# First mixer: steps in another order and banks dealt anew; second mixer: the last convolution taps behind the next tails

## What is computed

```python
h = _rmsnorm(x, norm_mix_pre)
z_a, z_b, z_c, z_d = _split(h @ w_in, GROUP_SPLITS)
y_a = _rwkv7(z_a, ...)   # 4 heads of 64: s = s*w + (s@-kk) x (kk*a) + v x k, y = s@r
y_b = _mlstm(z_b, ...)   # 4 heads, chunks of 64, gates from i_pre and f_pre
y_c = _swa(z_c, ...)     # window of 128, sinks, relative bias
y_d = _fox(z_d, ...)     # causal softmax with forgetting gates
x = x + _rmsnorm(concatenate([y_a, y_b, y_c, y_d]) @ w_out, norm_mix_post)
gate, up = split(_rmsnorm(x, norm_ffn_pre) @ ffn_w_up)
x = x + _rmsnorm((gelu(_causal_dwconv(gate)) * up) @ ffn_w_down, norm_ffn_post)
```

```python
q, k, v, g, a_lr, u, gate_b, gate_c = split(h @ w_in)
o = gla_chunked(q, k, v, logg) ...                    # four heads, chunks of 64
z = gate_b * causal_dwconv(gate_c * u, conv_w)        # three taps a channel
return concatenate([o, z]) @ w_out
```

## Time and profile before

| | |
|---|---|
| median of 3 runs | 1627.43 us |
| the profiled execution's own time | 1627.35 us |
| its span in the trace | 1625.6 us |
| PE busy | 1604.6 us (99%) |
| DVE busy | 823.2 us (51%) |
| ACT busy | 669.9 us (41%) |
| POOL busy | 266.4 us (16%) |
| chain that ended last | PE 95%, DVE 3%, DMA 1%, ACT 1%, issue 1% |

### The profile page before, as it was taken

One profiled execution on the slowest core, in us unless ns is written; L12 is line 12 of the kernel. 1 busy time (PEld: TensorE's weight loads), 2 busy tenths in 40 slices (PEclk: granted clock), 3 DMA queues, 4 the chain that ended last, 5 costly groups with the idle time before them and its releaser, 6 DMA issues.

```text
span 1625.6 us, 22612 instructions
## 1 busy us (share of the span) xinstructions
PE 1604.6 (99%) x8876; PEld 1318.4 (81%) x8876; DVE 823.2 (51%) x1403; ACT 669.9 (41%) x1227; POOL 266.4 (16%) x229
## 2 busy tenths in 40 slices
PE   9999999999999999999999999999999999999998
PEld 6776777888888888888888888878888888888887
DVE  6667557376555622374444433346775444443333
ACT  7556555464444333363333333244334433333222
POOL 1222122002222110002222210000020122222000
PEclk9999999999999999999999999999999999999999
DMA  5331100423323333223233332333223232332332
GB/s 189 93 92 41 54 27 14 145 89 104 96 88 101 101 94 98 85 90 104 91 101 94 99 96 85 110 102 104 66 79 104 91 104 91 96 99 89 95 106 75
DMA packets 45984, 149.59 MB, mean 92 GB/s; under 512 B 5260, under 2 KB 8500, under 8 KB 45880
## 3 DMA queue, kind: packets, MB, share of 16 engines
q1 hardware_dynamic: 41760, 142.10, 28.3%
q10 hardware_dynamic: 4120, 6.06, 1.1%
HBM read 146.03 MB, written 2.11 MB: 91 GB/s over the span
## 4 chain that ended last, share of the span: by engine, by line
PE 95%; DVE 3%; DMA 1%; ACT 1%; issue 1%; DVEq 0%; SPq 0%; ACTq 0%
PE bank L280 93%; PE bank L478 1%; DVE x L2324 1%; DVE lo L1829 0%; DMA raw<-in_w_in 0%; DVE x L2665 0%; DVE y L2319 0%; ACT hi L1116 0%; PE bank L530 0%; DMA raw<-in_ffn_w_gate 0%; PE bank L538 0%; DMA raw<-in_w_out 0%; DVE yf L2319 0%; DVE small L1962 0%; ACT sq L1250 0%
## 5 line engine op out<-in xcount | busy, mean ns | idle before, releaser
L1829 DVE TENSOR_TENSOR lo<-raw,hi 128x512 fp32r<-128x512 f32 (+1 forms) x514 | 393.7, 790 | 572.4 <-ACT hi L1116 572.2
L280 PE MATMUL bank<-xh,hi 128*128 128x512 f32 (+1 forms) x1640 | 618.2, 388 | 3.5 <-ACT xh L1528 1.3
L280 PE MATMUL bank<-xh,lo 128*128 128x512 f32 (+1 forms) x1640 | 608.2, 382 | 1.3 <-DVE lo L1829 1.2
L280 PE MATMUL bank<-xl,hi 128*128 128x512 f32 (+1 forms) x1592 | 598.3, 387 | 0.0
L1116 ACT ACTIVATE hi<-raw 128x512 fp32r<-128x512 f32 (+1 forms) x540 | 322.1, 616 | 423.2 <-PE bank L280 378.4
L280 PEld LDWEIGHTS bank<-xh,hi 128*128 128x128 f32 x1640 | 304.3, 189 | 72.3 <-issue 6.8
L280 PEld LDWEIGHTS bank<-xh,lo 128*128 128x128 f32 x1640 | 303.9, 189 | 61.7 <-DVE lo L1829 2.4
L280 PEld LDWEIGHTS bank<-xl,hi 128*128 128x128 f32 x1592 | 299.0, 188 | 63.1 <-issue 3.5
L280 PE MATMUL bank<-fH,hi 128*128 128x512 f32 (+1 forms) x572 | 213.8, 374 | 0.0
L280 PE MATMUL bank<-fH,lo 128*128 128x512 f32 (+1 forms) x572 | 213.3, 373 | 0.0
L280 PE MATMUL bank<-fL,hi 128*128 128x512 f32 (+1 forms) x572 | 213.3, 373 | 0.0
(11 more groups left out here) (420 smaller groups left out, 1072.5 us busy)
## 6 DMA issues: line engine op xcount, KB each, us to landing
raw<-in_ffn_w_up SPq DMA_DIRECT2D x88, 512.0 KB, 3.5
raw<-in_w_in SPq DMA_DIRECT2D x50, 512.0 KB, 3.5
raw<-in_ffn_w_down SPq DMA_DIRECT2D x48, 512.0 KB, 3.5
raw<-in_ffn_w_gate SPq DMA_DIRECT2D x44, 512.0 KB, 3.5
raw<-in_ffn_w_down SPq DMA_DIRECT2D x24, 384.0 KB, 3.1
raw<-in_w_out SPq DMA_DIRECT2D x16, 512.0 KB, 3.5
x<-in_xt SPq DMA_DIRECT2D x8, 256.0 KB, 6.2
x<-in_xt ACTq DMA_DIRECT2D x8, 256.0 KB, 5.2
```

The source lines that it names most:

```text
L280: return pe.matmul(out, w, x, start=start, stop=stop, skip_group_check=True)
L1829: dve.tensor_tensor(k.lo[i % CUT][:, 0:w], k.raw[u % RAW][:, at:at + w], k.hi[i % CUT][:, 0:w].bitcast(F), SUB).then_inc(k.cut_tail[i % 2], 1)
```

## The change

Two edits. The first writes `ORDER1` and `BANKS1` anew: the names occur as often as before, in another order, and the products take other banks. The second is in `vector_mixer2.proj`: the two taps of the convolution's last channel tile and the product behind them are not done right after its `cb`, but after the two next cuts of weight tails, in front of the tails of y. Lines behind it move by up to 7 in the last third of the file (L2481 becomes L2488, L2491 L2498, L2498 L2501, L2616 L2619, L2639 L2642).

```diff
 ORDER1 = """
-p p p p p p p p p p r1 p r0 p p p p a r0 p p p r0 p a a p r0 p p p r0 p a p a r0 p a r0 p p k0 k0 a p p r0 p a p p
+p p r1 p a p p p p p p p p p p p r0 p r0 p p r0 p r0 p a a p p a r0 p p p a p r0 p r0 p p r0 a p a p p r0 a a p p
...
 BANKS1 = {
-    "a": "6725656453761325675350645776721653376677565246524653572367456734245467533752567",
+    "a": "5663375235245217624343572674763443272473472462375203425715461743256562472173646",
...
+    def taps(i):
+        Y, cu = M.Y[4 + i], M.cu[i % 2]
+        dve.wait_ge(s.conv_act, i + 1)
+        stt(Y[:, :], cu[:, 1:T + 1], k.col("conv_w_2", 4 + i), Y[:, :], MUL, ADD).then_inc(s.conv_dve, 1)
+        dve.wait_ge(s.conv_dve, 2 * i + 1)
+        stt(Y[:, :], cu[:, 0:T], k.col("conv_w_2", i), Y[:, :], MUL, ADD).then_inc(s.conv_dve, 1)
+
...
-            if u >= 13 and part == 2:
-                Y, cu = M.Y[4 + i], M.cu[i % 2]
-                dve.wait_ge(s.conv_act, i + 1)
-                stt(Y[:, :], cu[:, 1:T + 1], k.col("conv_w_2", 4 + i), Y[:, :], MUL, ADD).then_inc(s.conv_dve, 1)
-                dve.wait_ge(s.conv_dve, 2 * i + 1)
-                stt(Y[:, :], cu[:, 0:T], k.col("conv_w_2", i), Y[:, :], MUL, ADD).then_inc(s.conv_dve, 1)
-                if i == 3:
-                    dve.wait_ge(s.conv_dve, 2 * i + 2)
-                    dve.wait_ge(*k.read_at(("in2", u)))
-                    dve.tensor_tensor(Y[:, :], Y[:, :], M.cb[i % 2][:, :], MUL).then_inc(s.conv_dve, 1)
+            if u >= 13 and part == 2 and i < 3:
+                taps(i)
             yield
         cut_tails(dve, k, 2 * (u0 + 25) + 5)
         yield
         cut_tails(dve, k, 2 * (u0 + 25) + 6)
+        taps(3)
+        dve.wait_ge(s.conv_dve, 8)
+        dve.wait_ge(*k.read_at(("in2", 24)))
+        dve.tensor_tensor(M.Y[7][:, :], M.Y[7][:, :], M.cb[1][:, :], MUL).then_inc(s.conv_dve, 1)
```

More of the change, by code:

```diff
@@ L59 @@
 ORDER1 = """
-p p p p p p p p p p r1 p r0 p p p p a r0 p p p r0 p a a p r0 p p p r0 p a p a r0 p a r0 p p k0 k0 a p p r0 p a p p
[L61 to L64, removed]
+p p r1 p a p p p p p p p p p p p r0 p r0 p p r0 p r0 p a a p p a r0 p p p a p r0 p r0 p p r0 a p a p p r0 a a p p
+p r1 k0 p p r0 a c0 r1 p c0 p c0 k0 r0 p p r0 r1 a p a c1 r1 p r0 c1 p a p a r1 p r1 r0 c1 c0 c0 a r1 p r0 a r1 r0
+a m r0 a p r0 r1 a r1 k1 k1 p r0 a r1 r0 c1 p m r1 r0 a p a r1 a c1 r0 k0 r0 p m r1 r0 m r0 r1 r0 r1 r0 k0 r1 m m
+r0 r1 m r0 m r1 m p r1 r0 r1 r0 m f00 r1 m f01 a r1 r1 a k1 m f01 p a k1 r1 m a p p m m r1 m r1 a a p m a a p f00
+m f10 p a s m s r1 f00 r1 r1 f10 f01 f11 a f10 m f11 a f11 m s s s s s s s a o o s o o o o o o o
 """.split()
 BANKS1 = {
-    "a": "6725656453761325675350645776721653376677565246524653572367456734245467533752567",
[L70 to L78, removed]
+    "a": "5663375235245217624343572674763443272473472462375203425715461743256562472173646",
+    "m": "642364034546376275626212",
+    "r0": "6257672545374674537753577233474551674253336556377475722",
+    "r1": "7623267563676235425762522645352465254154366531065564535",
+    "k0": "53457476",
+    "k1": "36716743",
+    "f00": "634",
+    "f01": "556",
+    "f10": "776",
+    "f11": "523",
 }
```

## The result

The changed kernel takes 1621.04 us in the median of 7 runs (1620.51 to 1624.8), the kernel before 1627.06 (7 runs). The ratio is 0.9967, interval [0.9957, 0.9976]. The 7 runs lie in two groups: five from 1620.51 to 1621.06 with a mean granted clock of 0.997 or 0.998, and two at 1624.68 and 1624.8 with 0.994. The profiled execution is one of the two (1624.8, span 1623.0). I read both, since the first shows what the clock does and the second what the change does.

A forecast was written before the change was run, and what follows sets the result against it. TensorE, busy 1604.6 of 1625.6 us, bounds the kernel, so only its waits, some 21 us, can move. -1.40 -0.8 -1.3 +0.5 +0 = -3.0 us against 1627.35 gives 1624.4, range 1621.6 to 1627.5.

The forecast's parts named there:

- a change too small to tell: Whole kernel: time between 1624.18 and 1630.68 us, a change within 0.2% (3.25 us); chance 0.54.
- most of the first mixer's waits go: First mixer: waits of 0.98, 2.5 and 1.3 go, no new ones, with -1.40: 1621.1 to 1623.2; chance 0.20.
- The second mixer, -1.40: Second mixer's end, 1210 us: `lo` directly follows `cb`, PE's lost 1.40 goes whole, the wait before `x` stays.
- The wait at 136, -0.8: First mixer, 136.31 us: another, long-read bank saves 1.0; a step next to its own predecessor gives 0.2 back.
- 144 to 169, -1.3: First mixer: two pieces brought in cover about half of some five waits; -1.3, bounds 0 and -2.5.
- 169 to 222, +0.5: First mixer: two pieces fewer; the gate rows' DMA makes PE wait near 195; +0.5, bounds 0 and +3.
- my -1.6: First mixer: -0.8 at 136, -1.3 in 144 to 169 and +0.5 in 169 to 222 together.
- 222 to 277, 0: First mixer: waits of at most 2.69 sit at other steps; value 0, bounds -1.3 and +1.3.
- the sign of being wrong that I had named: First mixer, 222 to 277 us: the prediction is wrong if idle time is off 2.7 by more than 1.3.
- The rule on the shared port: First mixer: GpSimd tails coming forward could hold up DVE operations with two SBUF inputs; worst case +0.9 for -1.3.
- The slower rival: First mixer, 191 to 204 us: about ten steps each find their bank 0.5 late; 1628.9, up to 1631; chance 0.07.

The follow-up runs named there:

- The moved gate-row step: The changed kernel with the gate-row step two recurrence steps earlier, PE's order word for word the same: 1619.84 us; repeated, 1619.69.
- The two spliced kernels: The changed kernel with only the first mixer's 71 late steps and banks new: 1631.23 us; with only the 154 early ones new: 1631.92.
- the second trace: The changed kernel, nothing edited, profiled again later: 1620.56 us, span 1618.8, an execution like the five usual runs.

## Why the prediction was right, and where it was off

**Direction and size.** I forecast 3.0 us less and put 0.54 on a change too small to tell. It is 6.0 less by the medians (0.6 of it may be a fall of the clock in the kernel before, as in its trace). That is the rival "most of the first mixer's waits go", which I gave 0.20 and a middle of 1622.1.

**The second mixer, -1.40.** Right: 1.37 in the changed kernel, 1.50 alone. The chain before `x` moved along.

**The wait at 136, -0.8.** Right in kind: the idle time of 130 to 144 fell from 0.98 to 0.08. By two digits of the bank table alone it was 1.05, of which 0.38 came back 10 us later, where I had allowed for 0.2.

**144 to 169, -1.3.** Right in kind, too small: the idle time fell by 1.96. Putting the two pieces back cost 1.2 and brought 1.7 of idle back. I counted the pieces as a cover for half of the waits; by the idle time they cover nearly all of them.

**169 to 222, +0.5.** The gate rows' wait was there, with the mechanism as forecast: a DMA of 4.95 us against the 5.08 that I took, and a stop of 0.56 to 0.78 against 0.4 to 0.5. The place was 2 to 3 us earlier than I said; I had left out of this term that the waits ahead of it go. The moved gate-row step shows its whole worth, 1.0. The idle time rose by 1.3 in all, where I had 0.5. This error and that of 144 to 169 (0.7 the other way) nearly cancel: the first 154 steps gave -1.38 against my -1.6, and that this is so close is luck.

**222 to 277, 0.** This is the step of the prediction that failed. I wrote "I have no row that decides between fewer and more" and took 0 with a bound of -1.3. The measured part is -2.8, and the window's idle time fell from 2.69 to 0.35. It is also the sign of being wrong that I had named, an idle time off 2.7 by more than 1.3. The bound itself was the mistake: the row gives 2.69 as what there is to lose, and I had no reason to stop at half. The two spliced kernels show that this goes with the 71 late steps and their banks, whatever is ahead of them, though up to about 232 us both run at the lower clock and show little of waits there. What in these steps does it, the order of the finish steps or the banks, no run here separates.

**The rule on the shared port.** GpSimd's tails did come forward, from 176.24 and 190.87 to 165.00 and 179.81 us, 1.28 to 1.29 each. They cost nothing that can be seen, and DVE's 17.63 us in 144 to 169 is less than the 18.70 of before. But they didn't put the rule to the test: what DVE does beside them (`masked<-bank,consts`, `reg<-bank,rB`, `fx<-bank,rB`) has one input in a bank. Where both inputs of DVE's operation lie in SBUF, the trace agrees with the rule. The longest `lo` of 100 to 320 us, 1.07 against 0.69 in the median, starts while GpSimd is at a product:

```profile
121.43 1.29 POOL L2779 TENSOR_TENSOR rkv<-rkv,pair 128x512 f32<-128x512 f32 x1 [6.13 <-DVE pair L1880]
...
122.20 1.07 DVE L1829 TENSOR_TENSOR lo<-raw,hi 128x512 fp32r<-128x512 f32 x1 [0.31 <-ACT hi L1116]
```

The 1774 ns of the earlier trace rows, at 114.55 in the kernel before, start while GpSimd is at a `lo` of its own (114.25, 1.53 us).

**The slower rival.** It priced late evictions at 0.5 us a step over ten steps. The steps from 192.9 on have four waits of at most 0.8. But its sum, some 4 us, came in two of the first seven runs by a way that I had not named: one stop, and then the clock. The same matmuls start 3.7 us later in the profiled execution than in the second trace from 205 us on.

## What to carry to other kernels

Where engines run one hand-set order, the order and the dealing of the buffers are one thing: a product that takes a bank that another product has just filled waits for a whole eviction, and the new banks without the new order cost 26 us here. In a list of stretches, an idle time that you can't assign is a bound on the gain as large as it is; don't halve it. And a transfer's issue is moved by what stands ahead of it in its own queue, not by what stands ahead of it in the matmul engine's list: look for the instruction that holds the queue, then move past that one.

## What the runs showed of the hardware that I had not expected

Stops of 0.6 to 0.9 us among short matmuls were followed, within about 3 us, by TensorE's lower level: 10 us of it in the profiled execution of the changed kernel (0.52 from 195 to 205) for 3.7 us, and 17 us in the spliced ones (0.50) for 7 to 8, the stops (0.84 and 0.85) left out. That is five to nine times the stop itself. It is not certain in each run: with the same kernel and the same stop the clock stayed at 1.00 in the second trace. The kernel before has such a fall too: its stop of 0.63 at 691.27 is followed by some 3 us of the lower level (0.83 from 690 to 700) for 0.6 us, and the profiled execution of the changed kernel has that stop, 0.64 at 690.65, without a fall. The kernel before has a longer stretch with more stops (0.26, 0.43 and 0.85 from 151 to 160) and its profile shows 1.00 there.

A transfer of one row spread over 128 partitions (256 KB) took 4.95 us from issue to landing, longer than the 3.34 of a 512 KB weight unit. It is the second of four such that go out within 1.4 us. By the page's list of DMA issues the first, `reg<-gate_rows`, took 3.3 and the last two 5.2, and the DMA engines were busy 0.97 of the stretch from 188 to 190 us. So a good part of the wait for the gate rows may be the four standing in each other's way; no run here has one alone.
